# Two transformer blocks with 32 experts on one core: expert turn reordered, context norm inside the next product, convolution multiplier last

## The chip, the core and the metric

One core of one Trainium2 chip runs the whole program; the metric is its device time in microseconds. The core has TensorE (PE, with its weight loads PEld), VectorE (DVE), ScalarE (ACT), GpSimd (POOL) and SyncE (SP), which issues the weight transfers. Each engine works through its own instruction list in order, and waits on semaphores.

## What is computed

256 tokens of width 1024, all in float32. Block one is adaLN, three attention branches and a mixture of 32 experts with the best 4 for each token; block two is two layers (five gated FFNs of width 2816, a neighbourhood attention with context and pooling, a short convolution). The parts that the change touches:

```python
# experts: for each expert e, over the tokens that chose it
hb = xb @ w1[e] + b1[e];  g, u = hb[:, :F], hb[:, F:]
g = minimum(g, 7);  u = clip(u, -7, 7)
y[e] = ((u + 1) * g * sigmoid(1.702 * g)) @ w2[e] + b2[e]      # added with the router's weight
# even mixer: context keys and values from the modulated norm of ctx
cn = rms_norm(ctx) * g * (1 + scale) + shift
k_c, v_c = split(cn @ w_in[:, 512:1536]);  attention over [window, context];  pooling beside it
# odd mixer
bg, cg, xin = split(h @ w_in);  z = cg * xin
y = (bg * (z[t-1] * w0 + z[t] * w1 + z[t+1] * w2)) @ w_out
```

## The kernel before

Weights stream through a ring of 8 slots of 128x2048 float32 (1 MB each). To keep float32 accuracy at the fast matmul rate, each slot is split: ACT rounds it into `w_high` (4 buffers, L898 for experts, L989 after them), DVE writes the remainder `w_low` in place of the ring slot (L2150, L2283), and PE multiplies both. So a slot goes SP transfer, ACT high, DVE low, PE; `high(j)` waits until PE has used slot j-4, and the transfer of slot j until it has used j-8.

**Expert turns.** A loop of 16 turns (`experts` on each engine) takes two experts each, 24 slots a turn: gate and up of expert 0 (slots 0 to 7), of expert 1 (8 to 15), down of expert 0 (16 to 19) and of expert 1 (20 to 23). A 17th, shorter turn (`over`, 12 slots) follows for the overflow of the busiest expert. DVE's list in a turn is: lows 3 to 10, `gate_half(0)`, lows 11 to 15, `up_half(0)` (it ends with `hid[0]`, which down 0 needs), lows 16 to 19, `gate_half(1)`, `select` (the 0/1 selection matrices of the next pair: 8 tensor_scalar, L2126 and L2127), lows 20, 21, `up_half(1)` (`hid[1]`), lows 22, 23, the next turn's 0, 1, 2, and `add_result` (two adds from PSUM, L2193). ACT's list has the highs in step, PSUM evacuations (`rows`, L905), two `swish` (L916) and the copies of the gathered tokens (L884). PE ends a turn with down 0, `gather_next` (both halves, L1465), down 1, `result(0)`, `result(1)` (L1529). PSUM has four places of two banks; `MOE_PLACES` says which unit takes which.

**After the experts.** `split_gemm` takes 3 matmuls of 128x256 for each product block; a full slot is 48 matmuls. `norm(n)` on PE (L1231, 16 matmuls in the records) sums squares that ACT wrote (L753, L756); it stands before `ffn0_out` (norm 4, context) and before `ffn1_out` (norm 5, tokens). `even_qk`, `even_vu`, then norm 6 and `even_ctx`; DVE's `norm2` scales (L1807), ACT's `split_h` rounds (L1002), DVE's `low_part` takes the remainder (L1815), and PE waits for it. The neighbourhood attention follows: v transposes (L1628), pooling map (L1638) and pooling (L1647), then 8 steps of scores (L1657), softmax on DVE and ACT, turn (L1674), out (L1683). The convolution block projects b, c, x as `conv0`, `conv1`, `conv2`; DVE first splits four slots past `conv2` (`low_parts(ahead_of("conv2"))`), then makes `conv_z = conv2 * conv_c` (L2397), three taps (L2406, L2410) and the product with b (L2414), and `conv_out` (L1130) reads it. `ahead_of(name, most)` says how many slots past a product ACT and DVE split before they go on, 4 unless told otherwise.

## Time and profile before

| | us |
|---|---|
| median of 3 runs | 3110.52 (3103.82, 3110.52, 8970.65) |
| the profiled execution | 3108.63 |
| its span, first to last instruction | 3106.5 |
| PE busy | 2827.1 (91%) |
| DVE busy | 2124.6 (68%) |
| ACT busy | 1531.3 (49%) |

The span is one execution's; 2.1 us of that execution's time lie around it. PE's share is an average over stages: in the expert turns, from 606 to 1728 us, DVE is as full as PE.

### The profile page before, as it was taken

Reading aid. Unit: us, or ns where it says so; the run is one execution under the profiler, and the core shown is the slowest. Engines: PE = TensorE matmul, PEld = TensorE weight load, DVE = VectorE, ACT = ScalarE, POOL = GpSimd, SP = SyncE. Lnnn points to the kernel's source line nnn. Section 1 sums busy time; section 2 is a strip of 40 time slices with the busy share of each in tenths; the row PEclk is TensorE's granted clock in tenths of the full one; section 3 lists DMA queues with packets and bytes.
Section 4 is the critical chain, followed back from the end, with each engine's and each line's share of the span. In section 5 each row is a group of like instructions: output and inputs, shape, how many; then the busy total and the mean of one; then the engine's idle time right before and its main releaser. Section 6 shows DMA issues by size and latency. Waiting matters only on the chain.

```text
span 3106.5 us, 43548 instructions
## 1 busy us (share of the span) xinstructions
PE 2827.1 (91%) x17548; PEld 2555.3 (82%) x17548; DVE 2124.6 (68%) x1902; ACT 1531.3 (49%) x1287; POOL 11.1 (0%) x7
## 2 busy tenths in 40 slices
PE   5998988899999999989999799999879999998998
PEld 5987877777777777777777699999868999997898
DVE  5345663899999999998899777676433664554354
ACT  0022211877777777777777444343342334432242
POOL 0000000000000000000000100000000000000000
PEclk8887886899999999999999899999989999999999
DMA  9663452788888888888888676776513774544462
GB/s 370 214 217 135 149 191 96 320 332 354 355 358 354 358 358 355 357 336 342 351 337 356 209 256 246 258 272 244 173 45 129 265 258 155 185 163 136 135 191 81
DMA packets 172402, 776.10 MB, mean 250 GB/s; under 512 B 12112, under 2 KB 37712, under 8 KB 121328
## 3 DMA queue, kind: packets, MB, share of 16 engines
q1 hardware_dynamic: 168352, 767.08, 65.6%
q10 hardware_dynamic: 3920, 7.11, 0.8%
q8 instruction: 103, 1.69, 0.2%
q14 instruction: 27, 0.22, 0.0%
HBM read 773.10 MB, written 1.05 MB: 249 GB/s over the span
## 4 chain that ended last, share of the span: by engine, by line
PE 66%; DVE 15%; issue 10%; ACT 6%; DMA 2%; DVEq 0%; ACTq 0%; SPq 0%
PE psum L1169 11%; PE psum L1171 11%; PE psum L1167 11%; PE psum L1492 8%; DVE w_low L2150 8%; PE psum L1130 7%; ACT w_high L898 4%; PE psum L1273 4%; PE psum L1529 4%; PE psum L1213 2%; DVE mod_sums L1753 2%; PE psum L1231 1%; DMA ring<-in_exp_w 1%; DVE arena L2169 1%; PE psum L1335 1%
## 5 line engine op out<-in xcount | busy, mean ns | idle before, releaser
L2150 DVE TENSOR_TENSOR w_low<-ring,w_high 128x2048 fp32r<-128x2048 f32 x396 | 882.4, 2287 | 60.6 <-ACT w_high L898 48.4
L898 ACT ACTIVATE w_high<-ring 128x2048 fp32r<-128x2048 f32 x396 | 736.9, 1907 | 133.4 <-PE psum L1492 131.3
L2283 DVE TENSOR_TENSOR w_low<-ring,w_high 128x2048 fp32r<-128x2048 f32 (+1 forms) x199 | 434.1, 2185 | 431.0 <-ACT w_high L989 429.3
L989 ACT ACTIVATE w_high<-ring 128x2048 fp32r<-128x2048 f32 (+1 forms) x199 | 363.7, 1830 | 597.0 <-PE psum L1171 507.2
L1167 PE MATMUL psum<-h_high,w_high 128*128 128x256 f32 x2144 | 611.0, 285 | 35.9 <-issue 34.0
L1169 PE MATMUL psum<-h_low,w_high 128*128 128x256 f32 x2144 | 614.4, 287 | 0.0
L1171 PE MATMUL psum<-h_high,w_low 128*128 128x256 f32 x2144 | 614.2, 286 | 0.0
L1167 PEld LDWEIGHTS psum<-h_high,w_high 128*128 128x128 f32 x2144 | 417.1, 195 | 38.3 <-issue 36.3
L1169 PEld LDWEIGHTS psum<-h_low,w_high 128*128 128x128 f32 x2144 | 411.8, 192 | 0.0
L1171 PEld LDWEIGHTS psum<-h_high,w_low 128*128 128x128 f32 x2144 | 409.4, 191 | 0.0
L1492 PE MATMUL psum<-w_high,xg 128*128 128x512 f32 x1056 | 343.1, 406 | 10.3 <-DVE w_low L2150 10.2
L1492 PE MATMUL psum<-w_low,xg 128*128 128x512 f32 x1056 | 333.5, 397 | 0.0
L1492 PE MATMUL psum<-w_high,hid 128*128 128x512 f32 x528 | 194.1, 452 | 98.5 <-DVE hid L2184 77.0
L1753 DVE SCALAR_TENSOR_TENSOR mod_sums<-ring,cs,mod_sums 128x1024 f32<-128x1024 f32 x203 | 266.3, 1326 | 4.8 <-DMA ring<-in_mod_w 0.4
L1167 PE MATMUL psum<-m_high,w_high 128*128 128x256 f32 x880 | 247.6, 281 | 0.0
L1492 PEld LDWEIGHTS psum<-w_high,xg 128*128 128x128 f32 x1056 | 193.8, 189 | 65.2 <-DVE w_low L2150 22.7
L1169 PE MATMUL psum<-m_low,w_high 128*128 128x256 f32 x880 | 247.2, 281 | 0.0
L1171 PE MATMUL psum<-m_high,w_low 128*128 128x256 f32 x880 | 247.2, 281 | 0.0
L1492 PEld LDWEIGHTS psum<-w_low,xg 128*128 128x128 f32 x1056 | 199.4, 189 | 48.7
L1492 PEld LDWEIGHTS psum<-w_high,hid 128*128 128x128 f32 x528 | 107.5, 215 | 133.3 <-issue 71.7
L1492 PE MATMUL psum<-w_low,hid 128*128 128x512 f32 x528 | 181.1, 426 | 0.0
L1167 PEld LDWEIGHTS psum<-m_high,w_high 128*128 128x128 f32 x880 | 165.8, 188 | 0.1
(260 smaller groups left out, 3393.7 us busy)
## 6 DMA issues: line engine op xcount, KB each, us to landing
ring<-in_exp_w SPq DMA_DIRECT2D x396, 1024.0 KB, 8.4
ring<-in_ffn_w SPq DMA_DIRECT2D x135, 1024.0 KB, 5.1
ring<-in_mod_w SPq DMA_DIRECT2D x96, 1024.0 KB, 5.2
ring<-in_ffn_w SPq DMA_DIRECT2D x40, 768.0 KB, 4.6
ring<-in_w_in SPq DMA_DIRECT2D x24, 1024.0 KB, 7.9
ring<-in_even_w_in SPq DMA_DIRECT2D x12, 1024.0 KB, 6.8
ring<-in_conv_w_in SPq DMA_DIRECT2D x12, 1024.0 KB, 4.9
ring<-in_w_branch SPq DMA_DIRECT2D x6, 1024.0 KB, 5.3
```

Source lines behind the costliest of these rows:

```text
L898: act.activation(high_ap(j, D), slot_ap(PLAN.moe_slot + j), ACT.Copy).then_inc(sem("expert_high_ready" + c.x), 1)
L989: act.activation(high_ap(m, cols), slot_ap(s, 2, cols), ACT.Copy).then_inc(sem("w_high_ready"), 1)
L1130: mm = pe.matmul(unit(u0 + j // 4)[:, (j % 4) * T:(j % 4 + 1) * T], w[:, k % 2, (c0 + j) * P:(c0 + j + 1) * P], rhs(k), start=(k == 0 and ...
L1167: pe.matmul(dst, wh[:, k % 2, cols], high[:, k, :], start=first, stop=False, skip_group_check=True)
L1169: pe.matmul(dst, wh[:, k % 2, cols], low[:, k, :], start=False, stop=False, skip_group_check=True)
L1171: mm = pe.matmul(dst, wl[:, k % 2, cols], high[:, k, :], start=False, stop=last, skip_group_check=True)
L1273: mm = pe.matmul(unit(u)[:, j * T:(j + 1) * T], w[:, k, j * P:(j + 1) * P], hT[:, k, :], start=(k == 0 and j == 0), stop=(k == DC - 1), sk ...
L1492: mm = pe.matmul(u[:, cols], x_parts(k), w[:, k % 2, cols], start=(k == 0 and w is wh), stop=(k == DC - 1 and w is wl), skip_group_check=True)
L1529: mm = pe.matmul(c.unit(name)[:, (k % 4) * T:(k % 4 + 1) * T], moe_buf(f"y_rows{e}")[:, k * P:(k + 1) * P], moe_buf(f"selT{e}"), start=(e ...
L1753: last = dve.scalar_tensor_tensor(part, w[:, k % 2, :], cond, part, ALU.mult, ALU.add)
L2150: dve.tensor_tensor(low_ap(PLAN.moe_slot + j, D), slot_ap(PLAN.moe_slot + j), high_ap(j, D).bitcast(F32), ALU.subtract).then_inc(sem("expe ...
L2283: dve.tensor_tensor(low_ap(s, cols), slot_ap(s, 2, cols), high_ap(m, cols).bitcast(F32), ALU.subtract).then_inc(sem("w_split"), 1)
```

## The change

- Expert turn, PE: half of the next gather, then `result(0)`, stand between down 0 and down 1; the other half of the gather follows down 1, then `result(1)`. New unit order and PSUM places.
- Expert turn, DVE: `gate_half(1)` goes ahead of low 19, `up_half(1)` ahead of lows 20 and 21; four lows of the next turn instead of three stand before `add_result`. `select` is 2 compares of a pair and 4 products, with one link between. ACT: high 20 ahead of `swish(1)`, `gathered(0)` ahead of high 23, `gathered(1)` after `rows down1`, three of the next highs before that and one after it. The overflow turn: lows 8 to 10 ahead of `gate_half(0)`.
- Norms 4 and 5 are summed inside `ffn0_out` and `ffn1_out`, after the first slot. Norm 6 is summed inside `even_vu`, from a buffer of its own (`ctx_scaled`); DVE scales into it, then runs `low_parts(ahead_of("even_vu"))`, then the four `low_part(6, ...)`; ACT's `split_h(6)` waits for the end of `even_vu` and stands before the evacuation of `even_vu`.
- Attention: `na_scores(0)` ahead of the v transposes; `na_exps(0)` ahead of the copy of `pool_map`, `na_soft(0)` ahead of pooling's output; no split of the next FFN's slots until after the attention.
- Convolution: order `conv1`, `conv2`, `conv0`; `conv0` with its halves last, its product read from PSUM by the final multiply; taps made before it.

```diff
-             "gather0", "gather1", "down1", "result", "resultb")
-MOE_PLACES = (0, 1, 2, 3, 0, 1, 2, 3, 0, 1, 2, 3, 2, 1)
+             "gather0", "down1", "gather1", "result", "resultb")
+MOE_PLACES = (0, 1, 2, 3, 2, 1, 0, 2, 3, 1, 1, 0, 3, 2)
...
@@ ACT, experts
                 high(c, 19)
                 selection_turned(1)
+                high(c, 20)
                 swish(1)
-                high(c, 20, 21, 22)
+                high(c, 21, 22)
                 rows("down0", "y_rows0", 1.0 / ALPHA)
+                c.await_unit(act, "gather0")
+                gathered(0, c.unit("gather0"), c.x)
                 high(c, 23)
-                for half in range(2):
-                    c.await_unit(act, f"gather{half}")
-                    gathered(half, c.unit(f"gather{half}"), c.x)
                 if not last:
-                    high(c, *NEXT_SLOTS)
+                    high(c, *NEXT_SLOTS[:-1])
                 rows("down1", "y_rows1", 1.0 / ALPHA)
+                c.await_unit(act, "gather1")
+                gathered(1, c.unit("gather1"), c.x)
+                if not last:
+                    high(c, *NEXT_SLOTS[-1:])
...
@@ ACT, even mixer
             projected("even_qk", (z2q, HD ** -0.5), (z2k[:, :, 0:T], 1.0))
-            projected("even_vu", (z2v[:, :, 0:T], 1.0), (z2u, 1.0))
             act.wait_ge(sem("x_ready"), 4)
             act.dma_start(pool_band, ins["pool_band"]).then_inc(sem("band_landed"), 16)
-            norm(6, cT, hT[:, :, :])
-            split_h(6)
-            projected("even_ctx", (z2k[:, :, T:2 * T], 1.0), (z2v[:, :, T:2 * T], 1.0))
+            norm(6, cT, ctx_scaled[:, :, :])
+            high_parts(ahead_of("even_vu", HIGHS - 1))
+            await_unit(act, U["even_vu"] + 1)
+            split_h(6, ctx_scaled)
+            projected("even_vu", (z2v[:, :, 0:T], 1.0), (z2u, 1.0))
+            projected("even_ctx", (z2k[:, :, T:2 * T], 1.0), (z2v[:, :, T:2 * T], 1.0), most=0)
...
@@ PE, experts
                 down(0, range(DC // 2, DC), 16)
-                gather_next()
+                gather_next(0)
+                result(0, False)
+                gather_taken(0)
                 down(1, range(DC), 20)
-                gathers_taken()
-                result(0, False)
+                gather_next(1)
                 result(1, True)
+                gather_taken(1)
...
@@ PE, split_gemm: after the products of the first slot
+                if between:
+                    between()
...
-            split_gemm("even_vu", DC, DC, h_high, h_low)
-            norm(6, hT)
+            split_gemm("even_vu", DC, DC, h_high, h_low, between=lambda: norm(6, ctx_scaled))
...
-            for n in range(3):
-                split_gemm(f"conv{n}", DC, DC, h_high, h_low, after_norm(9) if n == 0 else None)
+            for n in CONV_ORDER:
+                split_gemm(f"conv{n}", DC, DC, h_high, h_low, after_norm(9) if n == CONV_ORDER[0] else None,
+                           halves_last=n == CONV_ORDER[-1])
...
@@ DVE, select
-                for e in range(2):
-                    for b in range(TB):
-                        p_, g_ = col(512 + COLS_E * b + e), col(580 + COLS_E * b + e)
-                        dve.tensor_scalar(sel[:, b, e, :], slot_no, p_, None, ALU.is_equal)
-                        last = dve.tensor_scalar(selG[:, b, e, :, :], slot_no[:, None, :].broadcast_to([P, 2, CAP]),
-                                                 p_, g_, ALU.is_equal, ALU.mult)
+                for b in range(TB):
+                    of = pair_of(512 + COLS_E * b)[:, :, None].broadcast_to([P, 2, CAP])
+                    last = dve.tensor_tensor(sel[:, b, :, :], slots, of, ALU.is_equal)
+                done(last)
+                for b in range(TB):
+                    of = pair_of(580 + COLS_E * b)[:, :, None].broadcast_to([P, 2, CAP])
+                    for d in range(2):
+                        last = dve.tensor_tensor(selG[:, b, :, d, :], sel[:, b, :, :].bitcast(F32), of, ALU.mult)
...
@@ DVE, experts
-                low(c, 16, 17, 18, 19)
+                low(c, 16, 17, 18)
                 gate_half(1)
-
-                select(lambda at: small[:, bass.ds(c.columns + (at + 2), 1)], c.x)
-                low(c, 20, 21)
+                low(c, 19)
+                select(lambda at: small[:, bass.ds(c.columns + (at + 2), 2)], c.x, steps.link)
                 up_half(1)
-                low(c, 22, 23)
+                low(c, 20, 21, 22, 23)
                 if not last:
                     low(c, *NEXT_SLOTS)
                 add_result()
...
@@ DVE, even mixer
+            root(6, EPS2)
+            for part in range(H_PARTS):
+                for k in (2 * part, 2 * part + 1):
+                    last = dve.scalar_tensor_tensor(ctx_scaled[:, k, :], cT[:, k, :], mod2[:, 0, 4, k:k + 1, 1],
+                                                    rstd[:, 0, :], ALU.mult, ALU.mult)
+                last.then_inc(sem("h_whole"), 1)
             low_parts(ahead_of("even_vu"))
-            norm2(6, 0, 1, 1)
-            low_parts(ahead_of("even_ctx"))
+            for part in range(H_PARTS):
+                low_part(6, part, ctx_scaled, mod2[:, 0, 3, :, 1])
+            low_parts(ahead_of("even_ctx", 0))
...
@@ DVE, convolution: taps of four chunks at a time, then
             for part in range(DC // 2):
+                u = U["conv0"] + part // 2
                 y = conv_y[:, 2 * part:2 * part + 2, :]
-                dve.tensor_tensor(y, y, conv_b[:, 2 * part:2 * part + 2, :], ALU.mult).then_inc(sem("conv_ready"), 1)
+                if part % 2 == 0:
+                    await_unit(dve, u)
+                b = unit(u)[:, 512 * (part % 2):512 * (part % 2) + 512].rearrange("p (c t) -> p c t", c=2)
+                last = dve.tensor_tensor(y, b, y, ALU.mult)
+                last.then_inc(sem("conv_ready"), 1)
```

## Rows read from the trace of the kernel before

**Rows 1.** Groups of instructions by line: out<-in, shapes, count | busy us, mean ns | idle.

```profile
L2150 DVE TENSOR_TENSOR w_low<-ring,w_high 128x2048 fp32r<-128x2048 f32 x396 | 882.4, 2287 | 60.6 <-ACT w_high L898 48.4 <-DVE arena L2193 7.5 <-DVE mod_sums L2242 0.7
L898 ACT ACTIVATE w_high<-ring 128x2048 fp32r<-128x2048 f32 x396 | 736.9, 1907 | 133.4 <-PE psum L1492 131.3 <-DMA ring<-in_exp_w 1.8
L905 ACT ACTIVATE arena<-psum 128x1024 f32<-128x1024 f32 x99 | 100.2, 1013 | 19.6 <-PE psum L1492 19.6
L1002 ACT ACTIVATE h_high<-hT,mod 128x256 fp32r<-128x256 f32 x64 | 28.2, 499 | 34.5 <-DVE hT L1807 34.5
```

**Rows 2.** Chain that ended last: start us, us, what; down 1 stages (x32).

```profile
606.04 9.92 PE psum L1492 x32
...
1294.92 7.52 PE psum L1492 x32
...
1681.78 9.67 PE psum L1492 x32
```

**Rows 3.** Timeline of DVE, one expert turn: start us, us, line, [idle before].

```profile
908.18 1.23 DVE L2193 TENSOR_TENSOR arena<-psum,arena 128x1024 f32<-128x1024 f32 x1 [2.38 <-PE psum L1529]
...
911.63 17.71 DVE L2150 TENSOR_TENSOR w_low<-ring,w_high 128x2048 fp32r<-128x2048 f32 x8 [0.49 <-DVE arena L2193]
...
941.72 0.69 DVE L2169 TENSOR_TENSOR arena<-psum,vecs 128x512 f32<-128x512 f32 x1
...
944.90 8.90 DVE L2150 TENSOR_TENSOR w_low<-ring,w_high 128x2048 fp32r<-128x2048 f32 x4
953.72 0.68 DVE L2169 TENSOR_TENSOR arena<-psum,vecs 128x512 f32<-128x512 f32 x1
...
954.78 0.25 DVE L2126 TENSOR_SCALAR sel<-consts,small 128x64 fp32r<-128x64 f32 x1
...
957.37 4.49 DVE L2150 TENSOR_TENSOR w_low<-ring,w_high 128x2048 fp32r<-128x2048 f32 x2 [0.83 <-ACT w_high L898]
```

**Rows 4.** Timeline of PE, same turn: results, first gather matmuls, start of down 1.

```profile
902.80 7.07 PE L1529 MATMUL psum<-arena 128*128 128x256 f32 x32
...
956.94 0.33 PE L1465 MATMUL psum<-sel,h_nat_high 128*128 128x128 f32 x2
...
964.97 1.22 PE L1492 MATMUL psum<-w_high,hid 128*128 128x512 f32 x2 [4.35 <-DVE hid L2184]
```

**Rows 5.** Timeline of ACT, same turn: the swish of expert 1.

```profile
954.90 0.63 ACT L916 ACTIVATE arena<-arena 128x512 f32<-128x512 f32 x1 [7.33 <-DVE arena L2175]
```

**Rows 6.** Windows: us, busy PE, PEld, DVE, ACT, POOL, then PEclk, DMA share, GB/s.

```profile
893.00:903.00 10.00, 9.73 (x33) 7.78 (x34) 8.52 (x5) 6.41 (x4) 0.00 (x0) 0.77 0.46 172
...
933.00:943.00 10.00, 10.00 (x53) 8.37 (x52) 9.93 (x7) 10.00 (x7) 0.00 (x0) 1.00 1.02 424
```

**Rows 7.** Timeline of PE after the expert turns: waits, norms, attention, convolution.

```profile
1728.02 1.22 PE L1492 MATMUL psum<-w_high,hid 128*128 128x512 f32 x2 [7.43 <-DVE hid L2184]
...
1902.61 6.34 PE L1231 MATMUL psum<-hT,consts 128*128 128x256 f32 x16 [4.93 <-ACT hT L756]
...
2108.03 6.03 PE L1231 MATMUL psum<-hT,consts 128*128 128x256 f32 x16 [4.08 <-ACT hT L753]
...
2229.19 5.19 PE L1231 MATMUL psum<-hT,consts 128*128 128x256 f32 x16 [4.80 <-ACT hT L756]
...
2239.96 0.55 PE L1167 MATMUL psum<-h_high,w_high 128*128 128x256 f32 x1 [5.57 <-issue]
...
2268.80 2.73 PE L1628 MATMUL psum<-consts,arena 128*128 128x128 f32 x16 [3.33 <-ACT arena L1057]
...
2284.31 1.97 PE L1674 MATMUL psum<-consts,arena 128*128 128x128 f32 x8 [3.39 <-ACT arena L1084]
...
2360.51 3.79 PE L1231 MATMUL psum<-hT,consts 128*128 128x256 f32 x16
...
2863.41 29.69 PE L1130 MATMUL psum<-arena,ring 128*128 128x256 f32 x128 [14.95 <-DVE arena L2414]
```

**Rows 8.** Timeline of DVE in the convolution block.

```profile
2857.72 2.35 DVE L2397 TENSOR_TENSOR arena<-psum,arena 128x1024 f32<-128x1024 f32 x2
```

More of the change, by code:

```diff
@@ L1101, in _ @@
                 psum_free[u % 4], 1)
+            high_parts(ahead_of("even_ctx"))
             for n, e in ((7, 2), (8, 3)):
@@ L2371, in _ @@
             na_soft(0)
+            u = U["pool_out"]
+            await_unit(dve, u)
+            for g in range(4):
+                last = dve.tensor_scalar(cat[:, 4 + g, :], unit(u)[:, g * T:(g + 1) * T],
+                                         vec("pool_scale")[:, g:g + 1], None, ALU.mult)
+            free(last, u)
             for s in range(len(NA_STEPS)):
@@ L2381, in _ @@
                                        chunks(u, 2, HD), wide(stats[:, 2, s, 0:2], HD), ALU.mult), u)
+            low_parts(ahead_of("even_ctx"))
             finish(*add_to(xT, U["even_out"], mod2[:, 0, 5, :, 0]), "x_ready")
@@ L2387, in _ @@
             norm2(9, 1, 1)
-            low_parts(ahead_of("conv0"))
             low_parts(ahead_of("conv1"))
-            low_parts(ahead_of("conv2"))
+            low_parts(ahead_of("conv2", HIGHS - 1))
             dve.wait_ge(sem("conv_edges"), 2)
@@ L2398, in _ @@
                                        conv_c[:, 4 * half:4 * half + 4, :], ALU.mult), u)
+            low_parts(ahead_of("conv2"))
             taps = vec("conv_w").rearrange("p (n k) -> p n k", n=3)
-            for part in range(DC // 2):
-                two = range(2 * part, 2 * part + 2)
-                if part % 2 == 0:
-                    await_freed(dve, U["conv2"] + part // 2)
-                    await_freed(dve, U["conv0"] + part // 2)
-                for k in two:
+            for half in range(2):
+                four = range(4 * half, 4 * half + 4)
+                await_freed(dve, U["conv2"] + half)
+                for k in four:
                     last = dve.tensor_scalar(conv_y[:, k, :], conv_z[:, k, 0:T], taps[:, 0, k:k + 1], None, ALU.mult)
@@ L2408, in _ @@
                 for n in (1, 2):
-                    for k in two:
+                    for k in four:
                         last = dve.scalar_tensor_tensor(conv_y[:, k, :], conv_z[:, k, n:n + T], taps[:, n, k:k + 1],
@@ L2412, in _ @@
                     link(last)
+            for part in range(DC // 2):
+                u = U["conv0"] + part // 2
                 y = conv_y[:, 2 * part:2 * part + 2, :]
-                dve.tensor_tensor(y, y, conv_b[:, 2 * part:2 * part + 2, :], ALU.mult).then_inc(sem("conv_ready"), 1)
+                if part % 2 == 0:
+                    await_unit(dve, u)
+                b = unit(u)[:, 512 * (part % 2):512 * (part % 2) + 512].rearrange("p (c t) -> p c t", c=2)
+                last = dve.tensor_tensor(y, b, y, ALU.mult)
+                last.then_inc(sem("conv_ready"), 1)
+                if part % 2 == 1:
+                    dve.wait_ge(sem("conv_ready"), part + 1)
+                    dve.sem_inc(psum_free[u % 4], 1)
+            low_parts(ahead_of("conv0", BOUNDARY))
             finish(*add_to(xT, U["conv_out"], mod2[:, 1, 5, :, 0]), "x_ready")
```

145 lines of the change are left out of this document (70 added, 75 removed).

## Prediction, made before the changed kernel ran

> **What bounds the kernel now.** I read the table of lines first, then the chain, then the timelines engine by engine in the places that the diff touches.
>
> The expert turns are 1100 us of the span. The chain view shows 16 down-1 stages, the first at 606.04 and the last at 1681.78, so a turn takes (1681.78 - 606.04) / 15 = 71.72 us [rows 2]. What must DVE do in that time? Back to back, eight lows take 17.71 us, that is (17.71 - 2.29) / 7 = 2.20 us from one to the next [rows 1, 3]. 24 of them are 52.9. A `gate_half` runs from 953.72 to 954.78, 1.06 us, twice 2.1. An `up_half` runs from 941.72 to 944.90, 3.18 us, twice 6.4. `select` runs from 954.78 to 957.37 less the 0.83 waited, 1.76. The two adds with the loop's jump take 911.63 - 908.18 = 3.45, of which about 0.5 is a wait for the second result: 2.95. The sum is 66.1 us [rows 3]. DVE therefore idles 5.6 us a turn, and it idles at the turn's end: 2.38 for the results, 0.83 for a high, the rest after `hid[1]` and in the adds.
>
> Why there? PE ends the gather at 964.97 - 4.35 = 960.62 and waits 4.35 us for `hid[1]` [rows 4], because `up_half(1)` stands behind lows 20 and 21. The granted clock then drops: 0.77 over 893 to 903, against 1.00 in the middle of a turn [rows 6], and down 1 takes 9.67 to 9.92 us where one stage that kept the 2.4 GHz level took 7.52 [rows 2]. High 0 of the next turn waits for the slow down 1, and the adds wait for both `result`s, 7.07 us behind it [rows 4]. DVE is the floor, PE's late wait keeps the turn above it.
>
> After the experts PE is the bound, with single stalls: the three norms, the start of `even_ctx`, the start of the attention, and 14.95 us ahead of `conv_out` [rows 7].
>
> **The change, part by part. Expert turn.** I walk the new order from 944.90 (low 16), with the durations of before. Lows 16 to 18 end at 951.5. `gate_half(1)` to 952.6, low 19 to 954.8, `select`, `up_half(1)`.
>
> `select` has 6 tensor_tensor of 128 elements in place of 8 tensor_scalar. By the two sizes shown (0.68 us at 512, 2.287 at 2048: 1.04 ns an element) one lasts 0.28 [rows 1, 3]. The old eight overlap at 0.22 each. So the new six cost 1.3 with the same overlap and 1.8 with none and the link: I take 1.4, a saving of 0.35. The Trainium skill ("VectorE: DVE Perf Modes", section on the perf-mode tier table) says that float32 tensor_tensor stays at one element a cycle while tensor_scalar gets two, which speaks against this edit. By its formula, (128+151)/0.96 = 291 ns each, nothing would be saved here, and my forecast would be 6 us later.
>
> `hid[1]` is then ready at about 956.2 + 3.2 = 959.4, against 964.97 - 0.1. ACT must have swished: high 20 needs slot 16 used and ends near 951.3, the clamp comes at 952.6, so the 7.33 us that `swish(1)` waited [rows 5] become about 1, in time. PE: down 0 ends at 956.9 [rows 4], half a gather (32 matmuls from 956.94 to 960.62: 1.84 a half) to 958.8, `result(0)` (half of 7.07) to 962.3. Both stand where the 4.35 wait was. Low 20 is there at 961.6, so down 1 starts at 962.3 at the full clock and follows the lows (2.2 a slot against its own 7.52/4 = 1.88) to 970.1. Then half a gather and `result(1)` to 975.5.
>
> DVE does eight lows without a break, 959.3 to 977.0. Is each high there? Next 0, 1, 2 follow PE's use of 20, 21, 22 (964.2, 966.1, 968.0) by 1.9; next 3 stands behind `rows down1` and the last gather copy (1.0 each [rows 1]) and ends at 974.9, just when DVE comes to it. This is the tightest point. The results are ready at 975.5, before the adds. New waits: `gather0` for `select` (ready 0.5 before), down 1 for the copy of gather 0 (2.5 before), next turn's up0_turn for `gate_half(0)` (over 4 before). The next low 4 starts near 980.2; with before it was 911.63 + 2.20 + 71.72 = 985.55. So the walk gives 66.3 us a turn, on DVE's floor of 65.8. I take **66.5** for handovers that I rounded away: 5.2 us saved, times 16 = **83 us**. Bounds: 5.9 (the floor) gives 94; if next 3 and the highs stay 2 us late, 51.
>
> Overflow turn: PE waits 7.43 us for `hid` [rows 7]. One low fewer at its start saves 2.2. Lows 8 to 10 before `gate_half(0)` take the place of that wait and let PE finish up 0 ahead of it; by the same walk `hid` comes 4.8 earlier in all. I count **5**. First lows: one more before the loop, one fewer in it: 0.
>
> **Norms 4 and 5.** The first slot of the next product (about 5.7 us at 48 matmuls) covers waits of 4.93 and 4.08, and the norm runs at the full clock, 3.79 instead of 6.34 and 6.03 [rows 7]. Saved: 4.93 + 2.55 = 7.5, and 4.08 + 2.24 = 6.3. Queued behind is DVE, which stands in `root` until the norm is done, then splits slot 4; it comes to that about 4 us before PE needs it. Together **13.8**; without the clock's part 9.
>
> **Norm 6.** `even_vu` ended at 2229.19 - 4.80 = 2224.39; with the norm inside it ends at 2228.2. Before, `even_ctx` began at 2239.96 [rows 7]. Now ACT rounds h only after `even_vu`: 8 casts of 0.5 less overlap, 3.5. But DVE stands in `low_parts(ahead_of("even_vu"))`, which wants all four slots of `even_ctx`, and ACT makes the fourth high only after casts and two evacuations: 3.5 + 2.0 + 1.9, then low 2.3 and the first `low_part` near 1.0 [rows 1]. That is 10.7: start at 2238.9. The norm's wait is turned into a wait for a weight split. I count **1**; were the queue not so, 9.5.
>
> **Attention.** From the end of `even_ctx` (2268.80 - 3.33) to the first turn it took 18.8 us [rows 7]. Now: scores at 0 to 1.1, v transposes to 3.3, pooling map to 5.5, exps done by 7.1 (behind two copies), the map's copy to 8.1, pooling to 11.7, second scores to 12.8, turn. That is 6.0 sooner and without the wait of 3.39. The second step had run at the lower clock; 3 more. **9**, bounds 5 and 11. The highs moved behind the attention have the 29 us of `even_out` as cover.
>
> **Convolution.** DVE came to `conv_z` at 2857.72 [rows 8], stuck in lows of the next FFN, and PE waited 14.95. Now lows past `conv2` are `conv0`'s own, taps (under 10 us) run beside `conv0`'s 23, and the last halves leave 5.7 us for the product. PE goes on without a wait; the start of `conv_out` at the high level is worth 2.15, as for down 1 [rows 2]. **17**; bounds 14 and 17.5.
>
> **Sum.** 83 + 5 + 13.8 + 1 + 9 + 17 = 129. The profiled execution took 3108.6 (span 3106.5, 2.1 around it; the median is 1.9 above it): 3108.6 - 129 = **2980**, 4.1% less.
>
> **Rivals.** (a) The transfers become the bound. 24 slots of 128x2048x4 bytes are 25.2 MB, now 351 GB/s over a turn and 378 at 66.5. Where slots are free the queue moves 424 [rows 6], and ACT waited only 1.8 us for transfers in all [rows 1], which speaks against it; for it, the transfers are already full in mid-turn. If the mean cannot rise, the turn stays at 71.7 and only the 46 us outside the turns are left: 3063. The Trainium skill's "DMA: Bandwidth & Descriptors" (Specifications) gives about 358 GB/s of HBM for one core. By it a turn needs 70.3 us, and the time would be about 3040; the 424 of this trace speaks against that here.
> (b) The turn gains only in part: next 3's high, or down 1 at the low clock, delays DVE by 1.5 to 3 us. 68 to 69.5 us a turn gives 3004 to 3028.
> (c) Slower: between down 0 and the turn's end TensorE falls to 1.2 GHz and stays. That work is 3.7 + 7.07 + 7.52 = 18.3 us at the high level; doubled, PE's turn (71.7 less 4.35, 2.15 and some 1.5 of small waits: 63.7) becomes 82. 10.3 us more, 16 times, less 46: 3227. It decides from about 11 us at the low level. For it: the drop seen at 0.77 [rows 6]. Against it: that drop follows a wait of 4.35, and the walk leaves none over 1.3.
> (d) The reorder moves waits about and DVE's end stays: as (a), 3063.
>
> **Chances.** Forecast, 2955 to 3000: 0.65. (b), up to 3048: 0.19. (a) and (d): 0.10. (c) and anything else that ends above: 0.06. 2% is about what this kernel's measurement can tell from no change; that is below 3048, so faster 0.84, within 0.10, slower 0.06. The range that leaves out no more than 2 in 10 is **2955 to 3028**.
>
> **What would show it.** Down-1 stages 66.5 apart and without a `hid` wait; the clock near 1.00 all through a turn; DVE idle under 1 us; no wait at the `conv_out` start; norms 4 and 5 at 3.8; and a wait of about 10 us ahead of `even_ctx` that ends on DVE's `low_part`. The forecast is wrong if ACT waits for transfers several us a turn, or if DVE waits for the fourth next high.

## The result, and the profile after

The changed kernel took 2993.1 us against 3113.1 us for the kernel before (medians of runs on one chip), and the ratio is 0.9622 with a 95% interval of 0.9599 to 0.9645: 3.8% faster, 13 us above the forecast of 2980 and inside its range of 2955 to 3028. One of the four runs of the kernel before was a slow one of 8970.7 us, which the ratio leaves out (without it the median is 3110.5). The profiled execution had a span of 2986.1 us, against 3106.5.

The page of the changed kernel, with the span in 40 slices:

```profile
PEclk8978887799999999999999899999999999999999
GB/s 375 233 197 165 132 183 143 246 373 359 372 368 377 382 379 378 381 375 365 366 368 371 207 248 278 247 282 259 179 43 135 274 268 143 197 155 184 141 198 71
```

The expert turns fill slices 9 to 21: the granted clock is 0.9 or more in each, and the transfers move 359 to 382 GB/s.

A turn is counted from one start of down 1 to the next on TensorE's timeline. Before it was 71.72 us, in the mean of fifteen. Now nine of the fifteen take 67.1 us; they are called clean here. Three take 68.3 and one 67.6, each with a short fall of the granted clock, and two that follow one take 66.4. The mean is 67.28. TensorE in a clean turn (start of the next gather behind down 0, result 0, down 1, second half of the gather behind it):

```profile
799.98 0.33 PE L1474 MATMUL psum<-sel,h_nat_high 128*128 128x128 f32 x2
...
801.71 3.67 PE L1538 MATMUL psum<-arena 128*128 128x256 f32 x16
...
805.03 0.82 PE L1501 MATMUL psum<-w_high,hid 128*128 128x512 f32 x2
...
813.36 0.34 PE L1474 MATMUL psum<-sel,h_nat_high 128*128 128x128 f32 x2
```

Down 1 starts without a wait for `hid` and lasts 8.3 us (805.03 to 813.36), where [rows 2] had 9.67 and 9.92. It runs at the 2.4 GHz level (granted clock 1.00 over 805 to 813.5), but slower than the 7.45 us that the chain view has for it in three turns behind a fall: in a clean turn it follows DVE's lows.

The splits in the table of lines, which answer to [rows 1] (busy us, mean ns | idle before them):

```profile
L2161 DVE TENSOR_TENSOR w_low<-ring,w_high 128x2048 fp32r<-128x2048 f32 x396 | 882.0, 2285 | 39.8 <-ACT w_high L900 35.8
L900 ACT ACTIVATE w_high<-ring 128x2048 fp32r<-128x2048 f32 x396 | 736.7, 1906 | 92.3 <-PE psum L1501 90.5
```

The work is the same; only the idle time ahead of it went, 60.6 to 39.8 us on DVE. Of what is left, 35.8 us are waits for ACT's highs. The timeline of DVE through the same clean turn shows where (it answers to [rows 3]):

```profile
797.82 0.48 DVE L2134 TENSOR_TENSOR sel<-consts,small 128x128 fp32r<-128x128 f32 x2
...
802.44 15.50 DVE L2161 TENSOR_TENSOR w_low<-ring,w_high 128x2048 fp32r<-128x2048 f32 x7
818.15 2.29 DVE L2161 TENSOR_TENSOR w_low<-ring,w_high 128x2048 fp32r<-128x2048 f32 x1 [0.21 <-ACT w_high L900]
820.36 2.56 DVE L2204 TENSOR_TENSOR arena<-psum,arena 128x1024 f32<-128x1024 f32 x2
823.97 15.50 DVE L2161 TENSOR_TENSOR w_low<-ring,w_high 128x2048 fp32r<-128x2048 f32 x7 [1.04 <-ACT w_high L900]
...
843.04 8.90 DVE L2161 TENSOR_TENSOR w_low<-ring,w_high 128x2048 fp32r<-128x2048 f32 x4 [0.30 <-ACT w_high L900]
```

Seven lows in a row after `up_half(1)`, then 0.21 us for the fourth next high, the adds without a wait for results, 1.04 us ahead of low 4 of the next turn (0.49 of it is the loop's own jump, which the kernel before had too), and 0.30 later, also there before. That is 1.55 us in a clean turn. ACT at the same place:

```profile
815.29 1.02 ACT L886 ACTIVATE xg<-psum 128x1024 fp32r<-128x1024 f32 x1 [0.71 <-PE psum L1474]
816.22 1.90 ACT L900 ACTIVATE w_high<-ring 128x2048 fp32r<-128x2048 f32 x1
820.73 1.28 ACT L900 ACT_TABLE_LOAD   x1 [2.61 <-PE psum L1501]
822.02 5.52 ACT L900 ACTIVATE w_high<-ring 128x2048 fp32r<-128x2048 f32 x3
```

An ACT_TABLE_LOAD is the instruction with which ACT loads the table of a function; there are two in a turn, this one and one ahead of the first `swish`. In the kernel before the same load stood in time that ACT had to spare (the timeline of ACT of the kernel before):

```profile
904.04 1.28 ACT L898 ACT_TABLE_LOAD   x1
905.34 1.91 ACT L898 ACTIVATE w_high<-ring 128x2048 fp32r<-128x2048 f32 x1
911.78 3.79 ACT L898 ACTIVATE w_high<-ring 128x2048 fp32r<-128x2048 f32 x2 [4.53 <-PE psum L1492]
```

The load is bound to the top of the loop's body, ahead of the first high there. Before, that was high 3, for which ACT had to wait for nothing. The change took high 3 out of the body's start, so the first is high 4, whose slot PE frees late: the load now runs after a wait of 2.61 us and ahead of a high that DVE wants.

A turn with a fall of the clock, on TensorE at the start of down 0:

```profile
924.49 1.09 PE L1501 MATMUL psum<-w_high,hid 128*128 128x512 f32 x2 [1.25 <-DVE w_low L2161]
```

The granted clock was 0.66 over 924 to 929. TensorE's work behind it came later, and DVE's wait for the fourth next high was 0.71 us there instead of 0.21. The same wait of 1.25 us stands ahead of down 0 in clean turns (790.29) without a fall; what makes the difference is not shown.

Behind the turns, the places of [rows 7] on PE (overflow turn, norm 4, start of `even_ctx`, pooling, `conv_out`):

```profile
1652.98 1.22 PE L1501 MATMUL psum<-w_high,hid 128*128 128x512 f32 x2 [4.83 <-DVE hid L2195]
...
1831.29 3.61 PE L1240 MATMUL psum<-hT,consts 128*128 128x256 f32 x16
...
2151.09 0.55 PE L1174 MATMUL psum<-h_high,w_high 128*128 128x256 f32 x1 [10.16 <-DVE w_low L2297]
...
2184.82 6.76 PE L1668 MATMUL psum<-arena 128*128 128x256 f32 x16 [3.04 <-ACT arena L1098]
...
2748.46 27.79 PE L1137 MATMUL psum<-arena,ring 128*128 128x256 f32 x128
```

The two norms and `conv_out` have lost their waits. `even_ctx` has 10.16, as forecast. The pooling ran at the 1.2 GHz level: 6.76 us where its 16 matmuls take 3.72 at the high one.

### The profile page after: what moved, and what is told of

The parts are those of the page before. It is cut to its first block, busy times and chain, and to the rows that moved or that the text cites. A ratio compares the mean times of both kernels' runs of the same rounds, so it can differ in the third digit from the quotient of the medians.

```text
span 2986.1 us, 43531 instructions
## 1 busy us (share of the span) xinstructions
PE 2798.5 (94%) x17548; PEld 2511.3 (84%) x17548; DVE 2113.3 (71%) x1868; ACT 1530.7 (51%) x1285; POOL 9.9 (0%) x7
## 4 chain that ended last, share of the span: by engine, by line
PE 64%; DVE 19%; issue 13%; ACT 3%; DMA 0%; DVEq 0%; ACTq 0%; SPq 0%
PE psum L1176 12%; PE psum L1178 12%; PE psum L1174 12%; DVE w_low L2161 11%; PE psum L1137 7%; PE psum L1501 5%; PE psum L1282 4%; PE psum L1538 2%; ACT w_high L900 2%; PE psum L1222 2%; DVE mod_sums L1761 1%; PE psum L1474 1%; PE psum L1240 1%; DVE arena L2180 1%; PE psum L1344 1%
## 5 line engine op out<-in xcount | busy, mean ns | idle before, releaser
L2161 DVE TENSOR_TENSOR w_low<-ring,w_high 128x2048 fp32r<-128x2048 f32 x396 | 882.0, 2285 | 39.8 <-ACT w_high L900 35.8
L2297 DVE TENSOR_TENSOR w_low<-ring,w_high 128x2048 fp32r<-128x2048 f32 (+1 forms) x199 | 442.0, 2229 | 368.2 <-ACT w_high L994 366.2
L1761 DVE SCALAR_TENSOR_TENSOR mod_sums<-ring,cs,mod_sums 128x1024 f32<-128x1024 f32 x203 | 257.4, 1282 | 4.8 <-DMA ring<-in_mod_w 0.4
L1501 PE MATMUL psum<-w_high,hid 128*128 128x512 f32 x528 | 180.7, 424 | 27.6 <-DVE w_low L2161 20.1
L1501 PE MATMUL psum<-w_low,hid 128*128 128x512 f32 x528 | 170.4, 404 | 0.0
L1176 PEld LDWEIGHTS psum<-m_low,w_high 128*128 128x128 f32 x880 | 165.8, 188 | 0.1
```

The costliest lines, as they stand in the source:

```text
L1176: pe.matmul(dst, wh[:, k % 2, cols], low[:, k, :], start=False, stop=False, skip_group_check=True)
L1501: mm = pe.matmul(u[:, cols], x_parts(k), w[:, k % 2, cols], start=(k == 0 and w is wh), stop=(k == DC - 1 and w is wl), skip_group_check=True)
L1761: last = dve.scalar_tensor_tensor(part, w[:, k % 2, :], cond, part, ALU.mult, ALU.add)
L2161: dve.tensor_tensor(low_ap(PLAN.moe_slot + j, D), slot_ap(PLAN.moe_slot + j), high_ap(j, D).bitcast(F32), ALU.subtract).then_inc(sem("expe ...
L2297: dve.tensor_tensor(low_ap(s, cols), slot_ap(s, 2, cols), high_ap(m, cols).bitcast(F32), ALU.subtract).then_inc(sem("w_split"), 1)
```

## The experiments

The runs were made in three groups, each on a chip of its own beside the kernel before: changed_again, silu_first, ctx_split_after and hid_late; results_late, turn_only, tail_only and best; select_scalar, silu_fill, turn_fill and best_fill. Across groups the ratios are to be compared, not the times.

The sections of the profiled executions, from PE's timeline, in us (a section ends where the next begins; the attention begins where `even_ctx` ends). Each column is one execution:

| section | before | changed | turn_only | tail_only | silu_first | ctx_split_after | best_fill |
|---|---|---|---|---|---|---|---|
| start to first down 1 | 606.0 | 603.2 | 597.8 | 601.5 | 597.3 | 597.4 | 598.0 |
| fifteen turns | 1075.7 | 1009.2 | 1009.7 | 1075.7 | 999.5 | 1007.6 | 999.4 |
| last down 1 to FFN 0 | 79.7 | 76.3 | 75.7 | 79.1 | 76.4 | 75.0 | 76.5 |
| FFN 0 and 1 | 416.7 | 402.9 | 414.1 | 402.1 | 400.9 | 400.9 | 401.8 |
| even products | 87.4 | 85.2 | 87.7 | 83.6 | 84.6 | 74.5 | 74.0 |
| attention | 65.5 | 58.6 | 78.5 | 54.7 | 67.7 | 57.2 | 54.7 |
| `even_out`, FFN 2 | 245.8 | 245.5 | 246.0 | 242.8 | 246.0 | 245.6 | 243.0 |
| FFN 3 | 200.2 | 197.8 | 200.2 | 201.0 | 200.1 | 200.0 | 200.9 |
| convolution to the end | 329.5 | 307.2 | 327.7 | 309.4 | 310.1 | 310.1 | 311.0 |

**changed_again.** The changed kernel once more, beside the next three.

> The changed kernel itself, as the partner of the others of this call. Both theories: about 2988 us, most turns 67.1 us, single ones 68.3.

Measured: 2987.1 us, ratio 0.9608 (0.9568 to 0.9648), span 2984.8, turn 67.28. FFN 3 took 200.1 here and 197.8 in the first profile of the same kernel; so 2.3 us of the difference to before were never the change's.

**silu_first.** Silu's table is loaded ahead of high 4's wait, by an activation of one column:

```diff
                     rows("down0", "y_rows0", 1.0 / ALPHA)
                     return
 
+                act.activation(small[:, 690:691], ident[:, 0:1], ACT.Silu)
                 high(c, 4, 5, 6)
```

> Edit to the changed kernel: one ScalarE activation of one column with Silu at the top of the loop's turn, writing a column that nothing reads. Theory T (the table load at the loop's top stands on DVE's path, 1.28 us after the wait for slot 0): the load runs while ScalarE waits, swish needs none of its own, VectorE's waits of 1.04 and 0.31 us a turn go: turn 65.7 to 66.1, 16 to 22 us less in all. Rival D (the turn is held at 67.1 by transfers, 375 GB/s): turn stays at 67.1, less than 3 us in all.

Measured: 2983.6 us, ratio 0.9587 (0.9542 to 0.9631), span 2982.7, turn 66.63 in the mean and 66.55 where clean. ACT and then DVE around the loop's end:

```profile
1210.61 1.28 ACT L932 ACT_TABLE_LOAD   x1
...
1213.22 5.58 ACT L900 ACTIVATE w_high<-ring 128x2048 fp32r<-128x2048 f32 x3 [1.11 <-PE psum L1502]
```

```profile
1210.63 2.29 DVE L2162 TENSOR_TENSOR w_low<-ring,w_high 128x2048 fp32r<-128x2048 f32 x1 [0.22 <-ACT w_high L900]
...
1215.89 15.50 DVE L2162 TENSOR_TENSOR w_low<-ring,w_high 128x2048 fp32r<-128x2048 f32 x7 [0.49 <-DVE arena L2205]
```

The load stands in ACT's idle time, the `swish` needs none of its own any more, and DVE's wait for high 4 is gone; 0.49 of it, the loop's own jump, stays. A clean turn fell by 0.55 us, just what the wait had beyond the jump and less than half of the load's 1.28; the fifteen turns fell by 9.7 us. Theory T had the place right and the size too high: it named a turn of 65.7 to 66.1 and 16 to 22 us, since it took the jump for a part of the wait and expected the 0.31 to go, which stayed. It also answers rival (a): 25.2 MB in 66.63 us are 378 GB/s, so the transfers did not hold the turn at 67.1. But the kernel as a whole was only 3 us below changed_again, which the intervals do not tell from none, and in the profiles only 2.1, because the attention took 67.7 us instead of 58.6, and nothing in the attention was edited. The last runs take that up.

**ctx_split_after.** DVE's low of slot 4 of `even_ctx` is put behind the context's low parts:

```diff
-            low_parts(ahead_of("even_vu"))
+            low_parts(ahead_of("even_vu", HIGHS - 1))
             for part in range(H_PARTS):
                 low_part(6, part, ctx_scaled, mod2[:, 0, 3, :, 1])
+            low_parts(ahead_of("even_vu"))
```

> Edit to the changed kernel: VectorE splits three slots of even_ctx, then takes the four low parts of the context norm, then the fourth slot. Theory Q (the 10.2 us wait ahead of even_ctx is VectorE standing in the fourth slot's split): the wait falls to about 2 us, start of even_ctx 8 us earlier, 8 to 10 us less in all. Rival H (the wait is ScalarE's rounding after even_vu and its evacuations): 0 to 1 us less.

Measured: 2972.1 us, ratio 0.9575 (0.9529 to 0.9620), span 2968.4. ACT and DVE of the changed kernel ahead of `even_ctx`:

```profile
2140.97 3.30 ACT L1007 ACTIVATE h_high<-arena,mod 128x256 fp32r<-128x256 f32 x8 [3.84 <-PE psum L1178]
2144.17 1.91 ACT L1062 ACTIVATE arena<-psum 128x1024 f32<-128x1024 f32 x2
2145.98 1.90 ACT L994 ACTIVATE w_high<-ring 128x2048 fp32r<-128x2048 f32 x1
```

```profile
2147.91 2.29 DVE L2297 TENSOR_TENSOR w_low<-ring,w_high 128x2048 fp32r<-128x2048 f32 x1 [8.46 <-ACT w_high L994]
2150.12 3.25 DVE L1815 SCALAR_TENSOR_TENSOR h_low<-arena,mod,h_high 128x256 fp32r<-128x256 f32 x8
```

DVE of ctx_split_after, same place:

```profile
2131.23 3.28 DVE L1815 SCALAR_TENSOR_TENSOR h_low<-arena,mod,h_high 128x256 fp32r<-128x256 f32 x8 [2.46 <-ACT h_high L1007]
2137.25 2.29 DVE L2297 TENSOR_TENSOR w_low<-ring,w_high 128x2048 fp32r<-128x2048 f32 x1 [2.74 <-ACT w_high L994]
```

The low parts follow ACT's casts, and the weight's low comes after them. PE's wait fell from 10.16 to 1.96 us and `even_ctx` itself from 25.8 to 23.3, since the clock no longer fell: the even products took 74.5 us against 85.2. Theory Q named 8 to 10 us for the whole; the time is 15 us under changed_again, with intervals of the two ratios that overlap, and 10.7 us of it are shown in this section.

**hid_late.** In the changed kernel lows 20 and 21 stand ahead of `up_half(1)` again, as before; TensorE's new order stays.

```diff
                 select(lambda at: small[:, bass.ds(c.columns + (at + 2), 2)], c.x, steps.link)
+                low(c, 20, 21)
                 up_half(1)
-                low(c, 20, 21, 22, 23)
+                low(c, 22, 23)
```

> Edit to the changed kernel: lows 20 and 21 stand ahead of up_half(1) again; TensorE's new order stays. Theory V (the gain of the turn is that hid of expert 1 is ready earlier on VectorE, the floor): hid comes 4.4 us later, TensorE waits 0.8 to 1.5 us between result(0) and down 1, VectorE waits for the next highs: turn 68.5 to 70. Rival P (the gain is TensorE's work in the old wait and the clock it keeps): turn within 0.4 of 67.1.

Measured: 3004.0 us, ratio 0.9668 (0.9627 to 0.9708), turn 68.16, between the bounds of V (68.5) and P (67.5). TensorE waits 1.2 us around `result(0)`, as V had it, and DVE waits 1.25 us for the fourth next high instead of 0.21, which is the whole difference of the turn:

```profile
1094.27 2.29 DVE L2161 TENSOR_TENSOR w_low<-ring,w_high 128x2048 fp32r<-128x2048 f32 x1 [1.25 <-ACT w_high L900]
```

**results_late.** The opposite: `hid[1]` is made early, but TensorE does both gathers ahead of down 1 and both results behind it.

```diff
                 gather_next(0)
-                result(0, False)
+                gather_next(1)
                 gather_taken(0)
                 down(1, range(DC), 20)
-                gather_next(1)
-                result(1, True)
                 gather_taken(1)
+                result(0, False)
+                result(1, True)
```

> The changed kernel with both gathers ahead of down 1 and both results behind it, as before the change (the copies of the gathered tokens on ScalarE moved with them); hid is still made as early as in the changed kernel. It leaves out the filling of the place between down 0 and down 1 with a result. Theory W (the early hid alone removes the wait, the order on TensorE then matters little): a turn of 67.1 to 68. Theory Y (the order on TensorE carries most of it, as the run with the late hid suggests, which lost only 1.0 us of 4.6): TensorE waits for low 20 after the gathers, the results stand 7 us behind down 1, the adds come later, a turn of 69.5 to 71.5, and the clock falls again in the turn.

Measured: 3015.8 us, ratio 0.9711 (0.9684 to 0.9738), turn 68.88. DVE at the first low of a turn:

```profile
963.09 15.50 DVE L2161 TENSOR_TENSOR w_low<-ring,w_high 128x2048 fp32r<-128x2048 f32 x7 [3.00 <-ACT w_high L900]
```

Neither theory's turn was met: the mean of 68.88 lies between W (up to 68) and Y (from 69.5). Undoing the early `hid` costs 1.1 us of the 4.6 that a clean turn had gained, undoing TensorE's order 1.7 (from 67.1 to 68.2 and 68.8). The two cover for each other: with results to do, TensorE can bear a late `hid`, and with an early `hid` the results matter only because 7.07 us of them stand ahead of slot 0 of the next turn, so that high 4 comes 2 us later (3.00 for 1.04, while the 0.21 for the fourth next high is gone). With both undone, and the fourth next low with them, all 4.6 are gone; how the rest divides wasn't tried.

**select_scalar.** The changed kernel with the old `select` of eight tensor_scalar.

```diff
-            def select(pair_of, x, done):
+            def select(col, x):
...
+                for e in range(2):
+                    for b in range(TB):
+                        p_, g_ = col(512 + COLS_E * b + e), col(580 + COLS_E * b + e)
+                        dve.tensor_scalar(sel[:, b, e, :], slot_no, p_, None, ALU.is_equal)
+                        last = dve.tensor_scalar(selG[:, b, e, :, :], slot_no[:, None, :].broadcast_to([P, 2, CAP]),
+                                                 p_, g_, ALU.is_equal, ALU.mult)
```

> The changed kernel with the old select: eight tensor_scalar in place of the six tensor_tensor. The trace of the changed kernel has 1.44 us for the six, that of before 1.76 for the eight: a turn 0.3 us longer (67.4 where the others were 67.1), 5 us in all, 2992. If VectorE's floor does not bind there, because it waits 0.71 and 1.04 us a turn for ScalarE, the turn stays at 67.1 and the time at 2987. By the rule that tensor_scalar is the faster form for float32, it would be no longer than the changed kernel either.

Measured: 2986.9 us, ratio 0.9608 (0.9579 to 0.9636), the same as the changed kernel; clean turns 67.3 where it had 67.1. The table of lines for the new `select` (changed kernel) and the old one (this run):

```profile
L2139 DVE TENSOR_TENSOR arena<-sel,small 128x128 f32<-128x128 f32 x68 | 15.3, 286 | 2.3
L2134 DVE TENSOR_TENSOR sel<-consts,small 128x128 fp32r<-128x128 f32 x34 | 8.3, 284 | 0.0
```

```profile
L2135 DVE TENSOR_SCALAR arena<-consts,small 128x128 f32<-128x128 f32 x68 | 23.2, 342 | 0.0
L2134 DVE TENSOR_SCALAR sel<-consts,small 128x64 fp32r<-128x64 f32 x68 | 16.9, 249 | 0.0
```

A turn's new `select` lasts 1.44 us (797.82 in the clean turn above to 799.26, where `up_half(1)` starts), the old one 1.67 here. 0.2 us a turn is 3 us in all, below what the timing can tell.

**turn_only and tail_only.** The kernel before with the hunks of the expert turn alone (`MOE_PLACES`, `NEXT_SLOTS`, `experts`, `gather_next`, `select`), and with all the others alone.

> The kernel before with the hunks of the expert turn, the overflow turn and select alone; everything behind the turns is as before. Theory additive: the turn part alone is worth what the profiles showed for it, 2.8 ahead of the first down 1, 66.3 in the fifteen turns and 3.4 behind them, 72.5 us: 3108 - 72.5 = about 3036, ratio 0.977, and the turn 67.3 us as in the changed kernel. The rival: the parts help each other through the clock (a turn part that keeps TensorE busy lets the norms run at the full clock); then this kernel and the one with the rest alone fall short of the 121 us together, by more than 10 us.

> The kernel before with everything but the turn's hunks: norms 4, 5 and 6 inside products, scores ahead of the pooling, the convolution's order. Theory additive: 7.7 + 6.65 + 2.2 + 7.0 + 16.8 + 1.9 = 42 us from the sections of the two profiles, so about 3066, ratio 0.986; the turn stays at 71.7 us. By the forecast it would be 46. The rival of parts that help each other: 35 or less here.

Measured: turn_only 3042.7 us, ratio 0.9784 (0.9764 to 0.9803); tail_only 3065.0 us, ratio 0.9863 (0.9842 to 0.9884). That is 67 and 43 us, 110 together, where the whole change gave 118 and 122 (0.9622, 0.9608). By the times, then, 8 to 12 us are missing, about the 10 that the rival asked for; but each interval is 6 us or more to either side, so the lack is not clear of noise. In the profiled executions nothing is missing: the spans fell by 69.1 and 56.5, 125.6 together, against 120.4. (That of tail_only was its fastest, 3051.8 us, with 3062 to 3074 in the other three, so its column shows more than its median.) Section by section, the fifteen turns of 1009.7 and, in tail_only, FFN 0 and 1 of 402.1 are those of the changed kernel: these parts add up. The attention does not. In turn_only, whose code there is that of before, it took 78.5 us instead of 65.5; in tail_only 54.7 instead of the 58.6 of the changed kernel, with the same code. So it is one section whose duration differs from kernel to kernel without an edit.

**best, silu_fill, turn_fill and best_fill.** `best` has both moves, silu_first's and ctx_split_after's. In the other three, six matmuls a step are added to the attention. Each step of the attention has a place where PE waits 1.11 us for ACT's copy of the turned probabilities. The six are put there, ahead of the wait; their result is overwritten:

```diff
-                await_freed(pe, u)
+                turned = u
                 u = U[f"na_out{s}"]
                 open_unit(pe, u)
+                for n in range(6):
+                    pe.matmul(unit(u)[:, 0:P], ident, ident, start=True, stop=True)
+                await_freed(pe, turned)
```

> The changed kernel with both moves that shortened their place: Silu's table loaded once a turn in ScalarE's idle time, and low 4 of the context product behind the context's low parts. Additive from the two runs: 2987 - 10 (turns) - 8 to 12 (start of the context product) = 2965 to 2969. If the attention's steps fall to the low clock again, as in the run with the table load alone (6.8 instead of 5.2 us a step, 9 us), about 2972 to 2978.

> The kernel with the table load alone, in which the attention took 68.0 us, with six matmuls of 128x128 put into each step of the attention where TensorE waits 1.11 us for ScalarE's copy of the turned probabilities (their result is overwritten; no work is left out). Theory K (the clock follows TensorE's short waits in the attention, and where it falls is an accident of timing): with the waits filled the clock stays at the 2.4 GHz level, a step takes 5.2 to 5.3 us, the attention 57 to 60, the run 8 to 11 us less than the 2983.6 of that kernel: about 2974. Rival M (the low level is given by something else, and a busier TensorE makes it more frequent): steps of 6.8 to 7.3 us, no gain or up to 3 us more.

> The kernel with the turn's hunks alone, in which the attention, whose code is that of the kernel before, took 78.7 us against 65.8 there, with the same six matmuls a step. Theory K: the attention takes 64 to 67 us, and the time falls from 3042.7 to about 3030, which is where the turn part alone (72.5 us) had to bring it; the missing 6 to 13 us of that run are then the clock in the attention and no interaction of the parts. Rival M: 76 us or more in the attention, 3042 or more.

> The kernel with both moves and the six matmuls a step. There the attention ran at the 2.4 GHz level already (57.5 us). Theory K: nothing changes there, 57.5 to 59, the time within 3 us of the 2974.4 of the kernel with both moves; the fill costs nothing where nothing has to be mended.

The attention in the view of windows, silu_first and then silu_fill (us; busy PE, PEld, DVE, ACT, POOL; PEclk, DMA share, GB/s):

```profile
2158.80:2226.50 67.70, 54.08 (x281) 39.55 (x281) 21.17 (x44) 25.39 (x47) 0.00 (x0) 0.77 0.05 16
```

```profile
2158.70:2213.40 54.70, 50.02 (x378) 42.25 (x377) 21.16 (x44) 26.04 (x47) 0.00 (x0) 1.00 0.06 20
```

On PE's timeline, one step of silu_first (scores, turns, outputs) and the next one's scores, and the same of silu_fill, with the fill at L1689:

```profile
2189.17 2.08 PE L1634 MATMUL psum<-arena 64*128 64x512 f32 x4
2191.18 1.77 PE L1682 MATMUL psum<-consts,arena 128*128 128x128 f32 x8
2194.06 2.00 PE L1691 MATMUL psum<-arena 128*128 128x64 f32 x16 [1.11 <-ACT arena L1094]
2195.99 2.08 PE L1634 MATMUL psum<-arena 64*128 64x512 f32 x4
```

```profile
2185.87 1.13 PE L1634 MATMUL psum<-arena 64*128 64x512 f32 x4
2186.93 1.09 PE L1682 MATMUL psum<-consts,arena 128*128 128x128 f32 x8
2187.85 1.50 PE L1689 MATMUL psum<-consts 128*128 128x128 f32 x12
2189.19 1.94 PE L1694 MATMUL psum<-arena 128*128 128x64 f32 x16
2191.06 1.13 PE L1634 MATMUL psum<-arena 64*128 64x512 f32 x4
```

6.82 us a step (2189.17 to 2195.99) against 5.19 (2185.87 to 2191.06): scores and turns at 2.08 and 1.77 us are those of the 1.2 GHz level, 1.13 and 1.09 those of 2.4 GHz, and the level had fallen anew in every step. With the wait filled it doesn't fall. Measured: silu_fill 2972.9 us, ratio 0.9554 (0.9532 to 0.9575), attention 54.7; turn_fill 3025.1 us, 0.9721 (0.9694 to 0.9749), attention 63.7 where it was 78.5; best_fill 2968.9 us, 0.9538 (0.9518 to 0.9559), attention 54.7, where `best` had 57.2 and took 2974.4, 0.9565 (0.9549 to 0.9581). Theory K holds in each against rival M. The gain is clear of noise in turn_fill alone (0.9721 against 0.9784 of turn_only); in the other two the intervals overlap with those of the kernels without the fill. But the granted clock of the whole span, which every execution has, rose in all four of each: 0.950 to 0.953 in silu_first and 0.955 to 0.956 in silu_fill, 0.942 to 0.943 in turn_only and 0.948 to 0.950 in turn_fill, 0.952 to 0.956 in `best` and 0.956 to 0.958 in best_fill. K's numbers were too careful in all three: it had 57 to 60 us for the attention of silu_fill, 64 to 67 and 3030 us for turn_fill, and in `best` it took the attention to be wholly at the high level, which it was not (7 us of it were low). That the wait itself makes the clock fall is not shown: the fill adds six plain matmuls to a step of small products and transposes and closes the wait at the same time, and no run parts the two. The fill did not cost the step anything: 5.19 us is also the step of the kernels at the high level without it. The Trainium skill ("TensorE: Matmul & The Clock Gate", section "A second HAM failure mode: psum-queue depth-cycling") tells of short idles between groups of matmuls that make the gate swing between its two levels; by that rule, the trace agrees, with a level that fell in every step beside waits of 1.11 us.

In all kernels here with the new attention its duration goes with the time at the low level in it: 54.7 us with none (tail_only, hid_late, silu_fill, best_fill), 56.2 with 3 (select_scalar), 57.2 to 57.8 with 7 (ctx_split_after, `best`, results_late), 58.6 with 10, 67.7 with 31.

`best` was not faster than ctx_split_after alone by the timing (0.9565 and 0.9575, intervals that overlap), though its turns are shorter by 8 us in the profile; it was to take 2965 to 2969 us if the two moves added up. best_fill is the fastest of all: by the ratios (0.9538 against 0.9608 and 0.9622) 22 to 26 us below the changed kernel.

## Why the prediction was right, and where its terms were off

The forecast's terms beside the sections of the two profiles (us saved):

| term | forecast | measured |
|---|---|---|
| turns, overflow turn, to FFN 0 | 88 | 72.7 |
| norms 4 and 5 | 13.8 | 13.8 |
| norm 6 and the even products | 1 | 2.2 |
| attention | 9 | 6.9 |
| convolution with `conv_out` | 17 | 18.8 |
| not forecast: FFN 2 to 4 | 0 | 6.2 |
| sum | 129 | 120.5 |

The forecast was 8 us too high in the profiles, and it would have been 15 too high without luck: the 6.2 us of FFN 2 to 4 were forecast by nothing, and for 2.3 of them, in FFN 3, changed_again shows that they are not the change's.

**Turns.** The walk was right in its order and in its cause, and in a clean turn right to a few tenths. `hid[1]` stands 4.62 us behind the start of `select` (797.82 to 802.44; the walk had 4.6); down 0 ends 2.5 us ahead of `hid[1]` (799.98; the walk had 2.5); next high 3 ends 15.7 behind it (818.12; the walk had 15.5), and DVE waits 0.21 for it, where the walk left 0.2. TensorE waits for `hid[1]` no more, down 1 keeps the high level, and DVE does not wait for results. The bound went where the text had put it, onto DVE's list. That list without its waits is 66.0 us with the jump, where the sum had 65.8.

What the walk did not have is high 4: it followed each engine's list from 944.90 to the adds, stopped short of that high, and gave the table load no place at all. Its 0.55 us, with 0.30 that was there before and 0.21, make 67.1. The term of 66.5 us a turn was therefore sized too low by 0.6 in clean turns and by 0.8 in the mean, the rest being the turns in which the clock fell. silu_first is the proof for high 4: 0.55 us less in a clean turn.

The whole row is 15 us short: 11.5 in the fifteen turns, 2.4 ahead of the first down 1 (where the two profiles of the changed kernel themselves differ by 4.3), and 1.6 behind the turns. Of the signs that the prediction named, DVE's idle time is 1.55 us and not under 1, and DVE does wait for the fourth next high, which was to show the forecast wrong; at 0.21 us, and 0.71 behind a fall of the clock, it was too small for that.

About that load, the Trainium skill ("ScalarE activation tables: per-element evaluation and per-set limits", section on table sets in the compiler and the runtime) says that the compiler places the loads by block; by that rule, the trace agrees, with one at the first activation of the loop's body in each turn, at 1.28 us.

**Overflow turn.** 5 was forecast; the start of its down product came 5.65 us sooner behind the last down 1 (46.24 before, 40.59 after), and the wait for `hid` fell from 7.43 to 4.83 and did not go. 2.2 of it were given back in norm 2, at the low clock: from that product to FFN 0 it took 33.5 us before and 35.7 after, with no edit there.

**Norms 4 and 5.** The section has the forecast sum to the decimal, which is in part luck. The waits are gone and each norm takes 3.61 us at the high level, which makes 4.93 + 2.73 and 4.08 + 2.42, 14.2 together; and turn_only, without these hunks, has the section 2.6 us shorter than before too.

**Norm 6.** The wait turned onto DVE's queue, as the text had it: 10.16 us against the 10.7 worked out, with the steps 3.30, 1.91, 1.90 and 2.29 that were named. ctx_split_after is the proof and the remedy, worth 10.7 us in its section (the forecast's "were the queue not so, 9.5").

**Attention.** The order gives what was forecast when the clock lets it: 65.5 to 54.7, 10.8 us, in tail_only. In the changed kernel the pooling fell on a low stretch (6.76 us for 3.72). The assumption that failed is that the clock is low in the second step before and high everywhere after: it differs from kernel to kernel, with 13 us between the best and the worst case of the same code. That 6.9 lies within the bounds of 5 and 11 is in part luck.

**Convolution.** 16.9 us less up to `conv_out` and 1.9 in it, no wait ahead of it. The sum of 18.8 is above the bound of 17.5: 16.9 is 1.9 more than the wait of 14.95, and what that is stays open.

**Rivals.** (a) and (d) would have held the turn at 71.7; it is 67.1, and 66.55 with the load moved. The Trainium skill's figure of about 358 GB/s ("DMA: Bandwidth & Descriptors", Specifications) would have held it at 70.3, an estimate; the measurement, 375 GB/s over a turn and 378 in silu_first, decides against it as a limit on this kernel. (b) named next 3's high as a delay of 1.5 us or more; it was 0.21, and 0.71 behind a fall of the clock. (c) did not happen: the clock is 0.9 or more in every slice of the turns.

**select.** Forecast 1.4 us and a saving of 0.35 a turn; the new one takes 1.44, the saving against the old in its place is 0.23. The formula of the Trainium skill ("VectorE: DVE Perf Modes", section on the TRN2 errata) gives an estimate of 291 ns for one tensor_tensor of 128 elements, and the trace has 284 and 286. That nothing would be saved was an estimate of six one behind the other, 1.75 us; in the trace they overlap to 1.44, and the eight tensor_scalar that they replace, with means of 249 and 342 ns, take 1.67.

## What to carry to other kernels

When a step is moved over the top of a loop, follow every engine's list through the top, table loads with it: a load that cost nothing where ACT had time to spare cost 0.55 of its 1.28 us behind a wait. Where TensorE is the bound and waits a microsecond at every step, its clock is part of the duration, and here a few matmuls in the wait kept it high at no cost. Before one turn of a loop is read in detail, count how long all of them take and take a usual one: here six of fifteen differ from the rest. And parts that are measured alone add up only section by section; a section whose clock moves must be read for itself.

## What the runs showed of the hardware

The same code can run at two rates in the split products, at a granted clock of 1.00 in both. The spacing of DVE's lows in FFN 3, which follows TensorE slot by slot, in the changed kernel's first profile and then in changed_again:

```profile
2512.69 1.76 DVE L2297 TENSOR_TENSOR w_low<-ring,w_high 128x1536 fp32r<-128x1536 f32 x1 [2.02 <-ACT w_high L994]
2518.34 1.76 DVE L2297 TENSOR_TENSOR w_low<-ring,w_high 128x1536 fp32r<-128x1536 f32 x1 [3.89 <-ACT w_high L994]
```

```profile
2508.91 1.76 DVE L2297 TENSOR_TENSOR w_low<-ring,w_high 128x1536 fp32r<-128x1536 f32 x1 [2.13 <-ACT w_high L994]
2514.67 1.76 DVE L2297 TENSOR_TENSOR w_low<-ring,w_high 128x1536 fp32r<-128x1536 f32 x1 [4.00 <-ACT w_high L994]
```

5.65 us a slot in one execution, 5.76 in the other, 2.3 us over FFN 3; what sets it stays open. The section up to the first down 1 also moves by itself: 603.2 and 598.9 us in the two profiles of the changed kernel. The four executions of one kernel lie 5 to 23 us apart here, so a difference of that size between two profiles says nothing until it is found in a section.
